# Attention sums that come out negated, with their minimum as the exponentials' bias

## The chip, the cores and the metric

The kernel runs on one core of one Trainium2 chip. The metric is device time in microseconds (us) of one execution; the kernel before was timed in three runs. The profile and the trace are of one more execution, taken by the hardware profiler. TensorE is written PE, VectorE DVE, ScalarE ACT, GpSimd POOL and SyncE SP, as the profile does; PEld is TensorE's weight load.

## The reference, cut to what matters

The network is a first block (an RWKV-7 group and an mLSTM group side by side, then a gated feed-forward stage) and a second block of two layers, 1,024 tokens of 1,024 features, all in float32. The change lies in the second block's attention. Each layer projects its input into three branches: A, four heads with a forgetting bias; B, six heads of a mixture of dilated windows; C, six query heads in a window of 128 with a learned sink per head. For a block of 128 queries and one head each branch computes a softmax over keys:

```
A:  s = q.k * scale + c_q - c_k          (c = cumulative sum of log_sigmoid(gate), c_q is the same for a whole row)
B:  s = q.k * scale + log(number of patterns that reach this key), masked
C:  s = q.k * scale, masked to the window; the sink is one more column with no value
p = exp(s - max(s)) / sum(exp(s - max(s)))      y = p @ v
```

The branch outputs are gated, projected, mixed, projected again and added to the stream; a norm ends the network.

## The kernel before

All engines' programs are written by hand, with semaphores between them; nothing reorders them. Activations lie as eight tiles of 128 features by 1,024 tokens. A float32 product is made of three PE passes over split operands (`hH`, `hL`, `wH`, `wL`); POOL splits each weight slot that SP loads (lines 688 and 690), and line 943 is the product itself (`col_gemm`).

Each layer runs a gate stage (24 gate tiles in ten periods, PE line 1650, the weights' splits on POOL in lines 834 to 855), then the attention, then a merge. In the second gate period and the fourth the forgetting rows are made beside it by DVE in `gate_rows` and `gate_sums` (lines 3686 to 3703): four rows of 1,024 log-gates and their running sum, `lrows`, which ACT sends to memory; before the heads of branch A they are spread over all partitions into `cMe` and `cMo`, and `mask_bias` lays the causal mask on every second block.

The attention takes two heads at a time, a `head_pair`: two pairs of A, three of B, three of C in each layer, so 16 in all: 4 of A, 6 of B, 6 of C. A pair has eight query blocks n = 0 to 7 with two heads j = 0, 1, so 16 pieces. In A and B piece n is 128 queries by (n + 1) * 128 keys; in C it is 128 by 256 (128 for n = 0). For each n:

- PE: `scores(n)` (line 1740) makes the score products in PSUM banks 0 to 3. Before `scores(n)` PE waits on the semaphore `at_max` until both pieces of block n - 1 have been read, and for the tensors it reads. Through n = 3 and in C the first scores stand between pieces of the next weight products (line 943); for A and B, n = 4 to 7 stand by themselves, with `transposes` (line 1767) and `values` (line 1785).
- DVE: `maxima(n)` (line 3790 on). For each head one `tensor_tensor_reduce` (line 3811) adds the bias to the scores, writes the sums to `sc` and keeps their largest; on the chip it is two instructions, the sum itself and a read of the accumulator into `stat`. DVE then waits on `at_ttr` for its own read, and a 128x1 instruction turns the maximum into the bias of the exponentials: a multiplication by -1 (line 3818), in C with the larger of maximum and sink (line 3816). That instruction increments `at_max`.
- ACT: `exponentials(n)` (line 2689) waits for `at_max`, writes exp(sc + bias) in place and sums each row.
- PE transposes the exponentials into PSUM, ACT (`copy_transposed`, line 2709, in C line 2700) and DVE (line 3835, in C line 3828) copy them to `pt`, and PE multiplies them with the values. DVE does its share of the copies and the output gate (lines 3856 and 3861) between its sums, in the order written.

Of the kernel before, what the change touches and what calls it, by code (L numbers as in the profile page):

```python
# [20 lines left out]
ALU = mybir.AluOpType  # L21
ACT = mybir.ActivationFunctionType

P = 128
# [4 lines left out]
LAYERS = 2  # L29
# [62 lines left out]
VEC = {}  # L92
# [51 lines left out]
def build(nc, xin, vec, w_lora, consts, cmask, rope, lnm, band, ws, park, out):  # L144
    with ExitStack() as ctx:
# [36 lines left out]
        def sem(name):  # L182
            if name in LATER:
                name = LATER[name][0]
            if name not in sems:
                sems[name] = ctx.enter_context(nc.semaphore(name))
            return sems[name]
# [20 lines left out]
        pv = at("pv", EX, [P, NV_CHIP])  # L208
# [15 lines left out]
        def colr(name, k):  # L224
            return pv[:, bass.ds(VEC[name] + k, 1)]
# [161 lines left out]
        lnM = at("lnM", XA + 7 * TILE, [P, T])  # L387
# [3 lines left out]
        bandT = at("bandT", EX3 + 4 * TILE, [P, 2 * P])  # L391
        S_MAX, S_NEG, S_DEN, S_SINK, S_REC = range(5)
        stat = at("stat", EX3 + 4 * TILE + 2048, [P, 5, 16])
        rec_rows = at("rec_rows", EX3 + 4 * TILE + 2432, [16, P])
        recT = at("recT", YL, [P, KT, T])
        cM = [at("cMe", YH + 2 * TILE, [P, 2, T]), at("cMo", YH + 4 * TILE, [P, 2, T])]
# [65 lines left out]
        def bank(b, n=1):  # L462
            return ps[:, b:b + n, :].rearrange("p b n -> p (b n)")
# [1583 lines left out]
        def _(act):  # L2047
# [631 lines left out]
            def head_pair(br, L, i, first):  # L2679
                pi = L * 8 + i + first  # L2680
                last, even = pi * 16, pi * 8

                def exponentials(n):
                    c0, c1, _ = columns(br, n)
                    buf, b = (SC[0], band_slot(n)) if br == "C" else (SC[n % 2], 0)
                    for j in range(2):
                        s = 2 * n + j
                        act.wait_ge(sem("at_max"), last + s + 3)
                        act.activation(buf[:, j, b + c0:b + c1], buf[:, j, b + c0:b + c1], ACT.Exp,  # L2689
                                       bias=stat[:, S_NEG, s:s + 1], accum_out=stat[:, S_DEN, s:s + 1]  # L2690
                                       ).then_inc(sem("at_exp"), 1)

# [32 lines left out]
                else:  # L2725
                    slots = head_slots(L, br, i)
                    if br == "B":
                        act.wait_ge(gemm_done[0], slots[0][1] + 1)
                        raw = L * 14 + i * 2 + 2 * first
# [45 lines left out]
                if br == "C":  # L2775
                    act.wait_ge(sem("at_max"), last + 18)
                    act.sem_inc(sem("gate"), 1)
                    for j in range(2):
                        ins = act.activation(stat[:, S_SINK, j:16:2], stat[:, S_NEG, j:16:2], ACT.Exp,
                                             bias=colr("sink", L * 6 + i + 3 * j))  # L2780
# [52 lines left out]
        def _(dve):  # L2833
            own = Count(sem("dve_own"))
# [10 lines left out]
            st = Count(sem("m_step"))  # L2845
# [456 lines left out]
            M_STEPS = st.n  # L3302
# [381 lines left out]
                keys(L, 0)  # L3684

            def gate_rows(L):
                st = Count(sem("m_step"), L * 4 + M_STEPS)
                raw, work, ones = [r[0:4, :] for r in lrows]
                st.on(dve.memset(ones, 1.0))
                st.on(dve.tensor_tensor(raw, raw, grows[0:4, :], ALU.mult))  # L3690
                st.wait(dve)
                st.on(dve.tensor_scalar(raw, raw, pv[0:4, VEC["forget_b"] + L:VEC["forget_b"] + L + 1], None, ALU.add))
                st.wait(dve)
                dve.scalar_tensor_tensor(out=work, in0=raw, scalar=-1.0, in1=raw, op0=ALU.mult, op1=ALU.max
                                         ).then_inc(sem("gate_abs"), 1)
                return st

            def gate_sums(L, st):
                raw, work, ones = [r[0:4, :] for r in lrows]
                dve.wait_ge(sem("gate_log"), 2 * L + 4)  # L3700
                st.on(dve.scalar_tensor_tensor(out=raw, in0=raw, scalar=0.0, in1=work, op0=ALU.min, op1=ALU.subtract))
                st.wait(dve)
                dve.tensor_tensor_scan(work, ones, raw, 0.0, ALU.mult, ALU.add).then_inc(sem("gate_rows"), 1)

            def rope(L, n, a_raw, turned, source, rot, raw, dst):

# [44 lines left out]
            def head_pair(br, L, i, first):  # L3751
# [18 lines left out]
                def mask_bias():  # L3770

                    dve.wait_ge(sem("bB_ready"), 128 + (L * 2 + i + 1) * 64)
                    for q in range(2):
                        masked, bare = [rows[:, :, :].rearrange("p j (b e t) -> p e j b t", e=2, t=P)[:, q]
                                        for rows in (cM[q], cM[1 - q])]
                        dve.tensor_tensor(masked, bare, cst[:, C_NEG, :].unsqueeze(1).unsqueeze(1).to_broadcast([P, 2, KT // 2, P]),
                                          ALU.subtract).then_inc(sem("bias_masked"), 1)

                if br == "A" and i:
                    mask_bias()  # L3780
# [5 lines left out]
                def maxima(n):  # L3786

                    c0, c1, _ = columns(br, n)
                    buf, b = (SC[0], band_slot(n)) if br == "C" else (SC[n % 2], 0)
                    for j in range(2):  # L3790
                        s = 2 * n + j
                        if n >= buffers:

                            dve.wait_ge(sem("at_T"), pi * 16 + s + 1 - 2 * buffers)
                        dve.wait_ge(sem("at_S"), pi * 16 + s + 1)
                        if br == "A" and j == 0:
                            if n < 2:
                                dve.wait_ge(sem("bias_masked"), (L * 2 + i) * 2 + n + 1)
                            else:
                                dve.wait_ge(sem("bB_copied"), bias_copies(L, i) + n - 1)  # L3800
                        if br == "A":
                            bias, op = cM[n % 2][:, j, c0:c1], ALU.subtract
                        elif br == "B":
                            bias, op = lnM[:, P * (7 - n):P * (7 - n) + c1], ALU.add
                        else:
                            bias, op = bandT[:, c0:c1], ALU.add
                        mx = stat[:, S_MAX, s:s + 1]

                        dve.sem_inc(sem("gate"), 1)
                        o = score_bank(br, n, j)  # L3810
                        dve.tensor_tensor_reduce(buf[:, j, b + c0:b + c1], bank(0, 4)[:, o + c0:o + c1], bias, 1.0, -3e38, op,  # L3811
                                                 ALU.max, mx).then_inc(sem("at_ttr"), 1)
                        dve.wait_ge(sem("at_ttr"), pi * 16 + s + 1)
                        neg = stat[:, S_NEG, s:s + 1]
                        if br == "C":
                            ins = dve.tensor_scalar(neg, mx, colr("sink", L * 6 + i + 3 * j), -1.0, ALU.max, ALU.mult)
                        else:
                            ins = dve.tensor_scalar(neg, mx, -1.0, None, ALU.mult)  # L3818
                        ins.then_inc(sem("at_max"), 1)

                def copy_transposed(n):
                    c0, c1, _ = columns(br, n)
# [149 lines left out]
            def last_adds():  # L3972
# [30 lines left out]
                for e in range(KT):  # L4003
                    scale(1, e)

            for name, n in (("at_max", 2), ("at_y", 1), ("a_yL", 1), ("sg_ready", 1), ("sg_raw", 1)):
                dve.sem_inc(sem(name), n)
            for L in range(LAYERS):
# [170 lines left out]
```

## Time and profile before

| what | value |
|---|---|
| times of three runs | 3413.94, 3416.67 and 3421.68 us, median 3416.67 |
| span of the profiled execution, first to last instruction | 3412.5 us; its own time beyond the span is not recorded, the median lies 4.2 us above the span |
| PE busy | 3254.9 us, 95% |
| DVE busy | 1971.0 us, 58% |
| POOL busy | 1622.7 us, 48% |
| ACT busy | 1055.3 us, 31% |
| granted PE clock, mean | 0.985 |

Busy time is what an engine spends in instructions; the rest of the span it waits or issues. An engine with a share near the whole span can still lose time in its waits, and these the trace lists by the instruction that ended them. In the rows a start is in us from the span's first instruction, followed by the duration; `[1.35 <-DVE stat L3818]` means that the engine stood still for 1.35 us before this row and that the instruction on the right of the arrow ended it.

### The profile page before, as it was taken

The numbers are of one execution on the slowest core, as the hardware profiler recorded it, in microseconds if no ns is written. First come the engines' busy times: TensorE is split into PE (matmuls) and PEld (weight loads), VectorE is DVE, ScalarE is ACT, GpSimd is POOL, SyncE is SP. The second block draws the span as 40 slices with busy tenths as digits, with TensorE's granted clock in tenths as the row PEclk, the third lists the DMA queues.
The fourth block names the chain that finished last, engine by engine and source line by source line (L and its number), as shares of the span: only waits on it lengthen the run. The fifth ranks groups of instructions, "written<-read, shape, count | busy, mean of one in ns | idle before, by whom it ended". The sixth has DMA issues, their size and how long they took to land.

```text
span 3412.5 us, 55095 instructions
## 1 busy us (share of the span) xinstructions
PE 3254.9 (95%) x22070; PEld 2604.8 (76%) x22070; DVE 1971.0 (58%) x2678; ACT 1055.3 (31%) x1725; POOL 1622.7 (48%) x903
## 2 busy tenths in 40 slices
PE   7999789898999999999999999999999999999997
PEld 6878688687888888787877777678878877776786
DVE  7445644648877777883344554566752256444665
ACT  4212344223323333344332232320343233322301
POOL 3333334146777676657822222257478422222475
PEclk9999899999999999999999999999999999999998
DMA  3121100221111111112331211143223311111332
GB/s 137 44 91 44 56 4 4 85 83 53 53 55 41 54 55 55 50 62 99 143 107 44 56 52 47 38 163 121 99 105 106 119 45 50 43 44 50 136 124 87
DMA packets 88252, 247.68 MB, mean 73 GB/s; under 512 B 13072, under 2 KB 24048, under 8 KB 86144
## 3 DMA queue, kind: packets, MB, share of 16 engines
q1 hardware_dynamic: 69664, 189.34, 16.5%
q10 hardware_dynamic: 18400, 55.63, 5.0%
q8 instruction: 142, 2.33, 0.3%
q14 instruction: 46, 0.38, 0.0%
HBM read 191.28 MB, written 42.12 MB: 68 GB/s over the span
## 4 chain that ended last, share of the span: by engine, by line
PE 85%; DVE 8%; ACT 2%; issue 2%; POOL 2%; DMA 0%; DVEq 0%; POOLq 0%; SPq 0%; ACTq 0%
PE ps L943 30%; PE ps L1480 11%; PE ps L1650 9%; PE ps L1510 6%; PE ps L1934 5%; PE ps L1955 4%; PE ps L1740 3%; PE ps L1767 3%; PE ps L1785 3%; DVE sc L3811 2%; PE ps L1255 1%; PE ps L1533 1%; PE ps L1231 1%; PE ps L1618 1%; POOL unit_lo L834 1%
## 5 line engine op out<-in xcount | busy, mean ns | idle before, releaser
L688 POOL TENSOR_TENSOR wH<-wraw,pv 128x1024 fp32r<-128x1024 f32 x135 | 267.0, 1978 | 1221.5 <-PE ps L943 1097.7
L943 PE MATMUL ps<-hH,wH 128*128 128x512 f32 x1488 | 473.9, 400 | 26.3 <-DVE hL L3041 11.7
L943 PE MATMUL ps<-hL,wH 128*128 128x512 f32 x1488 | 466.6, 395 | 0.0
L943 PE MATMUL ps<-hH,wL 128*128 128x512 f32 x1488 | 465.2, 394 | 0.0
L3368 DVE TENSOR_TENSOR xT<-ps,xT 128x512 f32<-128x512 f32 x544 | 366.1, 690 | 60.9 <-PE ps L1510 54.8
L690 POOL TENSOR_TENSOR wL<-wraw,wH 128x1024 fp32r<-128x1024 f32 x135 | 353.7, 2620 | 10.6
L943 PEld LDWEIGHTS ps<-hH,wH 128*128 128x128 f32 x1488 | 274.5, 189 | 88.8 <-issue 17.9
L943 PEld LDWEIGHTS ps<-hL,wH 128*128 128x128 f32 x1488 | 277.8, 189 | 59.0 <-issue 1.7
L943 PEld LDWEIGHTS ps<-hH,wL 128*128 128x128 f32 x1488 | 277.7, 189 | 57.5 <-issue 0.3
L2689 ACT ACTIVATE sc<-sc,stat 128x256 f32<-128x256 f32 (+7 forms) x256 | 171.1, 669 | 163.1 <-DVE stat L3818 102.1
L1767 PE MATMUL ps<-cst,sc 128*128 128x128 f32 x900 | 148.7, 285 | 12.5 <-ACT pt L2709 8.4
L1767 PEld LDWEIGHTS ps<-cst,sc 128*128 128x128 f32 x900 | 97.0, 141 | 82.8 <-issue 60.7
L1740 PE MATMUL ps<-kP,qP 64*128 64x256 f32 (+3 forms) x672 | 131.6, 488 | 20.4 <-DVE stat L3818 16.6
L1650 PE MATMUL ps<-mixH,unit_hi 128*128 128x512 f32 x320 | 128.7, 402 | 14.5 <-POOL unit_lo L834 7.6
L1480 PE MATMUL ps<-mixH,unit_hi 128*128 128x512 f32 x336 | 133.8, 398 | 7.0 <-DVE ps L3483 4.1
L1480 PE MATMUL ps<-mixH,unit_lo 128*128 128x512 f32 x336 | 132.7, 395 | 0.0
L1480 PE MATMUL ps<-mixL,unit_hi 128*128 128x512 f32 x336 | 132.7, 395 | 0.0
L1650 PE MATMUL ps<-mixL,unit_hi 128*128 128x512 f32 x320 | 127.9, 400 | 0.0
L1650 PE MATMUL ps<-mixH,unit_lo 128*128 128x512 f32 x320 | 127.7, 399 | 0.0
L1785 PE MATMUL ps<-pt,vtok 128*64 128x128 f32 x1800 | 126.5, 280 | 0.0
L1510 PE MATMUL ps<-gL,wH 128*128 128x512 f32 x320 | 126.5, 395 | 0.0
L1510 PE MATMUL ps<-gH,wH 128*128 128x512 f32 x320 | 124.6, 389 | 0.0
(545 smaller groups left out, 7244.0 us busy)
## 6 DMA issues: line engine op xcount, KB each, us to landing
wraw<-ws SPq DMA_DIRECT2D x158, 512.0 KB, 3.5
gates<-gated SPq DMA_DIRECT2D x48, 512.0 KB, 2.7
sg<-gates SPq DMA_DIRECT2D x16, 1536.0 KB, 6.5
upA<-ws SPq DMA_DIRECT2D x42, 256.0 KB, 3.3
upB<-ws SPq DMA_DIRECT2D x42, 256.0 KB, 2.6
gateA<-ws SPq DMA_DIRECT2D x40, 256.0 KB, 3.5
gateB<-ws SPq DMA_DIRECT2D x40, 256.0 KB, 2.7
xT<-park ACTq DMA_DIRECT2D x2, 4096.0 KB, 12.1
```

Of the source, the lines that this page charges most:

```text
L688: pool.tensor_tensor(wH[:, j, :], wraw[:, j, :], zero, ALU.add).then_inc(w_hi, 1)
L690: pool.tensor_tensor(wL[:, j, :], wraw[:, j, :], wH[:, j, :], ALU.subtract).then_inc(w_ready[j], 1)
L943: mm = pe.matmul(pair(p)[:, half * HALF:(half + 1) * HALF], wp, hp[:, k, half * HALF:(half + 1) * HALF], start=(m == 0 and n == 0), stop=( ...
L1480: mm = pe.matmul(bank(b), wp, xp[:, k0 + k, c0:c0 + HALF], start=(start and k == 0 and n == 0), stop=(k == 3 and n == 2), skip_group_check ...
L1510: mm = pe.matmul(pair((2, 3, 1)[e % 3])[:, half * HALF:(half + 1) * HALF], w[:, 1, e * P:(e + 1) * P], h[:, half * HALF:(half + 1) * HALF] ...
L1650: mm = pe.matmul(bank(banks[b]), wp, xp[:, k0 + k, c0:c0 + HALF], start=(start and k == 0 and m == 0), stop=(k == 3 and m == 2), skip_grou ...
L1740: mm = pe.matmul(outs[j][:, c:e], qP[r, n * P:(n + 1) * P], kP[r, k0 + c - c0:k0 + e - c0], start=True, stop=True)
L1767: mm = pe.transpose(out[:, c:c + P], (SC[0] if br == "C" else SC[n % 2])[:, j, b + c:b + c + P], ident)
L1785: mm = pe.matmul(out[r, :], vtok[:, v + 64 * j:v + 64 * j + 64], pt[:, j, b + c:b + c + P], start=(c == c0), stop=(c + P == c1))
L1934: mm = pe.matmul(pair(p)[:, half * HALF:(half + 1) * HALF], wp, hp[:, k, half * HALF:(half + 1) * HALF], start=(k == k0 and n == 0), stop= ...
L2689: act.activation(buf[:, j, b + c0:b + c1], buf[:, j, b + c0:b + c1], ACT.Exp, bias=stat[:, S_NEG, s:s + 1], accum_out=stat[:, S_DEN, s:s + ...
L3368: ins = dve.tensor_tensor(x, bank(2 * pairs[e % len(pairs)] + half), x, ALU.add)
```

## The change

Every sum is multiplied by -1 as it is made, and the reduction keeps the minimum of the negated sums, which is the negated maximum. It goes straight to the `stat` column that the exponentials read as their bias, and the instruction that makes it increments `at_max`; the 128x1 instruction behind it and the wait on `at_ttr` are gone. The exponential is given a scale of -1. In C the minimum starts from the negated sink, read from a column of `pv`; those 12 columns are filled once, before the first layer. In A the bias was subtracted; since all branches now add, the forgetting rows are multiplied by -1 after their running sum, one 4x1024 instruction in each layer behind the scan, and the mask is added instead of subtracted.

```diff
--- before.py
+++ after.py
@@ -2686,7 +2686,7 @@
                     for j in range(2):
                         s = 2 * n + j
                         act.wait_ge(sem("at_max"), last + s + 3)
-                        act.activation(buf[:, j, b + c0:b + c1], buf[:, j, b + c0:b + c1], ACT.Exp,
+                        act.activation(buf[:, j, b + c0:b + c1], buf[:, j, b + c0:b + c1], ACT.Exp, scale=-1.0,
                                        bias=stat[:, S_NEG, s:s + 1], accum_out=stat[:, S_DEN, s:s + 1]
                                        ).then_inc(sem("at_exp"), 1)
 
@@ -3684,7 +3684,7 @@
                 keys(L, 0)
 
             def gate_rows(L):
-                st = Count(sem("m_step"), L * 4 + M_STEPS)
+                st = Count(sem("m_step"), L * 5 + M_STEPS)
                 raw, work, ones = [r[0:4, :] for r in lrows]
                 st.on(dve.memset(ones, 1.0))
                 st.on(dve.tensor_tensor(raw, raw, grows[0:4, :], ALU.mult))
@@ -3700,7 +3700,9 @@
                 dve.wait_ge(sem("gate_log"), 2 * L + 4)
                 st.on(dve.scalar_tensor_tensor(out=raw, in0=raw, scalar=0.0, in1=work, op0=ALU.min, op1=ALU.subtract))
                 st.wait(dve)
-                dve.tensor_tensor_scan(work, ones, raw, 0.0, ALU.mult, ALU.add).then_inc(sem("gate_rows"), 1)
+                st.on(dve.tensor_tensor_scan(work, ones, raw, 0.0, ALU.mult, ALU.add))
+                st.wait(dve)
+                dve.tensor_scalar(work, work, -1.0, None, ALU.mult).then_inc(sem("gate_rows"), 1)
 
             def rope(L, n, a_raw, turned, source, rot, raw, dst):
 
@@ -3774,7 +3776,7 @@
                         masked, bare = [rows[:, :, :].rearrange("p j (b e t) -> p e j b t", e=2, t=P)[:, q]
                                         for rows in (cM[q], cM[1 - q])]
                         dve.tensor_tensor(masked, bare, cst[:, C_NEG, :].unsqueeze(1).unsqueeze(1).to_broadcast([P, 2, KT // 2, P]),
-                                          ALU.subtract).then_inc(sem("bias_masked"), 1)
+                                          ALU.add).then_inc(sem("bias_masked"), 1)
 
                 if br == "A" and i:
                     mask_bias()
@@ -3799,24 +3801,17 @@
                             else:
                                 dve.wait_ge(sem("bB_copied"), bias_copies(L, i) + n - 1)
                         if br == "A":
-                            bias, op = cM[n % 2][:, j, c0:c1], ALU.subtract
+                            bias = cM[n % 2][:, j, c0:c1]
                         elif br == "B":
-                            bias, op = lnM[:, P * (7 - n):P * (7 - n) + c1], ALU.add
+                            bias = lnM[:, P * (7 - n):P * (7 - n) + c1]
                         else:
-                            bias, op = bandT[:, c0:c1], ALU.add
-                        mx = stat[:, S_MAX, s:s + 1]
+                            bias = bandT[:, c0:c1]
+                        least = colr("qkw", L * 6 + i + 3 * j) if br == "C" else 3e38
 
                         dve.sem_inc(sem("gate"), 1)
                         o = score_bank(br, n, j)
-                        dve.tensor_tensor_reduce(buf[:, j, b + c0:b + c1], bank(0, 4)[:, o + c0:o + c1], bias, 1.0, -3e38, op,
-                                                 ALU.max, mx).then_inc(sem("at_ttr"), 1)
-                        dve.wait_ge(sem("at_ttr"), pi * 16 + s + 1)
-                        neg = stat[:, S_NEG, s:s + 1]
-                        if br == "C":
-                            ins = dve.tensor_scalar(neg, mx, colr("sink", L * 6 + i + 3 * j), -1.0, ALU.max, ALU.mult)
-                        else:
-                            ins = dve.tensor_scalar(neg, mx, -1.0, None, ALU.mult)
-                        ins.then_inc(sem("at_max"), 1)
+                        dve.tensor_tensor_reduce(buf[:, j, b + c0:b + c1], bank(0, 4)[:, o + c0:o + c1], bias, -1.0, least, ALU.add, ALU.min,
+                                                 stat[:, S_NEG, s:s + 1]).then_inc(sem("at_max"), 1)
 
                 def copy_transposed(n):
                     c0, c1, _ = columns(br, n)
@@ -4003,6 +3998,9 @@
                 for e in range(KT):
                     scale(1, e)
 
+            own.on(dve.tensor_scalar(pv[:, VEC["qkw"]:VEC["qkw"] + 6 * LAYERS], pv[:, VEC["sink"]:VEC["sink"] + 6 * LAYERS],
+                                     -1.0, None, ALU.mult))
+            own.wait(dve)
             for name, n in (("at_max", 2), ("at_y", 1), ("a_yL", 1), ("sg_ready", 1), ("sg_raw", 1)):
                 dve.sem_inc(sem(name), n)
             for L in range(LAYERS):
```

On DVE, branch A, block n = 4 and the start of n = 5, before (the `ISA` rows are the sum and the read of its accumulator):

```order
L3811 ISA sc_185,stat<-ps,cMe 128x640 [waits bB_copied,at_T,at_S]
L3811 ISA stat 128x1
L3818 TENSOR_SCALAR stat<-stat 128x1 [waits at_ttr]
L3811 ISA sc_185,stat<-ps,cMe 128x640 [waits at_T,at_S]
L3811 ISA stat 128x1
L3818 TENSOR_SCALAR stat<-stat 128x1 [waits at_ttr]
L3811 ISA sc_186,stat<-ps,cMo 128x768 [waits bB_copied,at_T,at_S]
```

and in the changed program:

```order
L3813 ISA sc_185,stat<-ps,cMe 128x640 [waits bB_copied,at_T,at_S]
L3813 ISA stat 128x1
L3813 ISA sc_185,stat<-ps,cMe 128x640 [waits at_T,at_S]
L3813 ISA stat 128x1
L3813 ISA sc_186,stat<-ps,cMo 128x768 [waits bB_copied,at_T,at_S]
```

The second sum now stands directly behind the first one's read; all other DVE instructions of the pair keep their order. PE, ACT and SP have the same instructions in the same order as before, POOL too but for line numbers.

On DVE in the gate stage, behind the third gate period of each layer, the difference:

```order
 L3701 SCALAR_TENSOR_TENSOR fraw<-fraw,lrows_219 4x1024
 L3703 SCALAR_TENSOR_TENSOR lrows_219<-lrows_220,fraw 4x1024
+L3705 TENSOR_SCALAR lrows_219<-lrows_219 4x1024
 L3639 TENSOR_TENSOR ps<-ps,ecopy 128x512
 L3644 TENSOR_TENSOR gated_214<-ps,grows 128x512
```

The added row waits for the scan above it (line 3703); below it follow the copies of the next gate period.

## Rows read from the trace of the kernel before

**Rows 1.** First part of the page: busy time, share of the span, instructions of each engine.

```profile
PE 3254.9 (95%) x22070; PEld 2604.8 (76%) x22070; DVE 1971.0 (58%) x2678; ACT 1055.3 (31%) x1725; POOL 1622.7 (48%) x903
```

**Rows 2.** Waits of PE, whole span: who waited for whom, us in total, times, longest.

```profile
PE ps L1740 <- DVE stat L3818: 16.6, 21, 1.4
...
PE ps L1740 <- DVE stat L3816: 3.4, 12, 0.4
...
PE ps L943 <- DVE stat L3816: 1.0, 4, 0.3
```

**Rows 3.** PE in order of time, a B pair of the first layer, blocks 5 and 6.

```profile
1926.36 1.56 PE L1740 MATMUL ps<-kP,qP 64*128 64x512 f32 x8 [1.35 <-DVE stat L3818]
...
1929.49 0.77 PE L1767 MATMUL ps<-cst,sc 128*128 128x128 f32 x5 [0.87 <-ACT pt L2709]
1930.57 1.77 PE L1740 MATMUL ps<-kP,qP 64*128 64x512 f32 x8 [0.30 <-DVE stat L3818]
```

**Rows 4.** DVE in order of time, the same B pair, block 4.

```profile
1924.17 0.82 DVE L3811 CUSTOM_DVE_ANT_0 sc<-ps,lnM 128x640 f32<-128x640 f32 x1 [0.65 <-PE ps L1740]
1924.92 0.08 DVE L3811 DVE_READ_ACCUMULATOR2_ANT stat<- 128x1 f32 x1
1925.04 0.15 DVE L3818 TENSOR_SCALAR stat<-stat 128x1 f32<-128x1 f32 x1
1925.29 0.82 DVE L3811 CUSTOM_DVE_ANT_0 sc<-ps,lnM 128x640 f32<-128x640 f32 x1
...
1926.15 0.15 DVE L3818 TENSOR_SCALAR stat<-stat 128x1 f32<-128x1 f32 x1
```

**Rows 5.** DVE in order of time, an A pair, block 4, between its two sums.

```profile
1772.86 0.08 DVE L3811 DVE_READ_ACCUMULATOR2_ANT stat<- 128x1 f32 x1
...
1773.17 0.82 DVE L3811 CUSTOM_DVE_ANT_0 sc<-ps,cMe 128x640 f32<-128x640 f32 x1
```

**Rows 6.** DVE in order of time, one instruction in front of the sum behind it (B pair).

```profile
1905.97 1.23 DVE L3718 TENSOR_TENSOR vtok<-ps,pv 128x1024 f32<-128x1024 f32 x1 [4.99 <-PE ps L1708]
1907.11 0.28 DVE L3811 CUSTOM_DVE_ANT_0 sc<-ps,lnM 128x128 f32<-128x128 f32 x1
```

**Rows 7.** DVE in order of time, a C pair, block 1, from the first read on.

```profile
2144.66 0.08 DVE L3811 DVE_READ_ACCUMULATOR2_ANT stat<- 128x1 f32 x1
2144.78 0.21 DVE L3816 TENSOR_SCALAR stat<-stat,pv 128x1 f32<-128x1 f32 x1
2144.94 0.42 DVE L3811 CUSTOM_DVE_ANT_0 sc<-ps,bandT 128x256 f32<-128x256 f32 x1
...
2145.41 0.21 DVE L3816 TENSOR_SCALAR stat<-stat,pv 128x1 f32<-128x1 f32 x1
```

**Rows 8.** PE in order of time, the same C pair.

```profile
2145.68 0.70 PE L1740 MATMUL ps<-kP,qP 64*128 64x256 f32 x4 [0.26 <-DVE stat L3816]
```

**Rows 9.** The chain that ended last, in the same C pair (start, us, what).

```profile
2156.18 0.60 ACT pt L2700
```

**Rows 10.** DVE by line: count, busy us, mean ns of one, idle before.

```profile
L3818 DVE TENSOR_SCALAR stat<-stat 128x1 f32<-128x1 f32 x160 | 24.6, 154 | 5.7
...
L3816 DVE TENSOR_SCALAR stat<-stat,pv 128x1 f32<-128x1 f32 x96 | 20.6, 214 | 3.4
```

**Rows 11.** DVE in order of time, first layer's gate stage, the scan and what follows.

```profile
1585.98 3.27 DVE L3703 TENSOR_TENSOR_SCAN lrows<-lrows,fraw 4x1024 f32<-4x1024 f32 x1
1591.53 0.70 DVE L3639 TENSOR_TENSOR ps<-ps,ecopy 128x512 f32<-128x512 f32 x1 [2.29 <-PE ps L1650]
```

**Rows 12.** One source line of DVE: ns of one, min/median/max, first and last start.

```profile
L3692 DVE TENSOR_SCALAR fraw<-fraw,pv x2: 1628/1628/1629, 1532.5 to 2504.3; 4x1024 f32<-4x1024 f32 x2
```

**Rows 13.** POOL in order of time, beside the scan of rows 11.

```profile
1587.22 3.10 POOL L834 TENSOR_TENSOR unit_lo<-gateB,unit_hi 128x512 fp32r<-128x512 f32 x1
...
1592.32 1.30 POOL L834 TENSOR_TENSOR unit_lo<-unit_sum,unit_hi 128x512 fp32r<-128x512 f32 x1 [0.74 <-ACT unit_hi L2541]
```

**Rows 14.** The chain that ended last, same gate stage (start, us, what).

```profile
1566.95 59.85 PE ps L1650 x252
```

## Prediction

> **What bounds the kernel now.** The page's first lines come first: PE is busy for 95% of the span, every other engine for 58% or less [rows 1]. So a microsecond saved on DVE counts only where PE stands still for it. The second view is therefore PE's list of waits. Three of its entries end with the instruction that the change removes [rows 2]: `scores` waits for line 3818 (A and B) 21 times, 16.6 us; `scores` waits for line 3816 (C) 12 times, 3.4 us; the product that follows a C pair's scores waits for line 3816 four times, 1.0 us. Together 21.0 us, 0.6% of the span: the change can't win more from these waits, however much work it takes from DVE. The third view is PE and DVE in order of time at such a wait, to see how much of it goes.
>
> In a B pair PE waits 1.35 us before `scores(5)`, 0.87 us for ACT's copy before the second `transposes(4)`, and 0.30 us before `scores(6)` [rows 3]. The ten pairs of A and B all repeat this, so 20 of the 21 waits are these two: 10 x (1.35 + 0.30) = 16.5 of the 16.6 us. The last one is some tenths at most, and I leave it out.
>
> **What is removed: 256 small instructions and their waits.** Line 3818 takes 154 ns 160 times, line 3816 takes 214 ns 96 times [rows 10]: 45 us of DVE, most of it beside a busy PE. What counts is one step: the two sums of a block, from PE's scores to the `at_max` that lets PE go on.
>
> B [rows 4]. The first sum's read starts at 1924.92, the negation 0.12 later, the second sum another 0.25 later: 0.37 from read to sum. With the negation gone the second sum needs only the engine. How soon can it follow? In [rows 6] a sum starts 0.09 us before the instruction in front of it has ended (1905.97 + 1.23 = 1907.20 against 1907.11), although the same semaphore instruction stands between them. So I take it that the second sum starts as the read ends, 0.08 after its start: 0.29 saved. The dear end is that it follows the read as it now follows the negation, 0.25 after: 0.12 saved. Behind the second sum `at_max` comes at the end of the negation, 1926.15 + 0.15 = 1926.30, and PE starts at 1926.36; it will come at the end of the read. The read stands 0.12 ahead of the negation and takes 0.08, so it ends at 1926.11: 0.19 saved. One B step: 0.48, dear end 0.31.
>
> A [rows 5]. From read to sum 0.31, to become 0.08: 0.23 saved, dear end 0.12; and 0.19 at the end. One A step: 0.42, dear end 0.31.
>
> Now the sum over PE's waits. The wait before `scores(5)` is longer than a step's saving, so all of that arrives: 4 x 0.42 + 6 x 0.48 = 4.6 us. The copy that PE waits for next starts from transposes behind `scores(5)`, so this wait moves along and stays as long as it was. Before `scores(6)` DVE is ready two steps earlier (0.84 to 0.96), PE one step earlier (0.42 to 0.48); the difference covers the 0.30 that PE waits, and the wait disappears: 10 x 0.30 = 3.0 us. What is late next there is PE itself, its transposes. From there PE runs on through `scores(7)`, and the gain stays. A and B: 4.6 + 3.0 = 7.6 us; dear end 3.1 + 3.0 = 6.1.
>
> C [rows 7]. From read to sum 0.28, to become 0.08: 0.20. At the end the negation runs to 2145.41 + 0.21 = 2145.62, the read, 0.12 ahead of it and 0.08 long, to 2145.37: 0.25. But the sum now reads its starting value, the sink, from a column, which no sum in the trace does. The nearest rows are the two small instructions, one with such a column and one without: 214 against 154 ns [rows 10]. I charge 0.06 per sum: a step saves 0.33 (dear end 0.06 + 0.19 = 0.25; free end 0.45). In each C pair PE waits three times. Before `scores(2)` it is about 0.25 us [rows 8], all of it gained: 6 x 0.25 = 1.5 us. Before `scores(6)`, the other six waits, 1.9 us in all, nothing: behind them PE needs exponentials that ACT makes after a copy, and that copy starts from PE's transposes in front of `scores(6)` (the chain of waits runs through it, [rows 9]). PE would only wait there instead. The last wait, in four of the six pairs, 1.0 us [rows 2], lies behind the last sums and goes: 1.0 us. C: 2.5 us, dear end 2.4, free end with the other six 4.4.
>
> **What is added.** The forgetting rows get one 4x1024 instruction in each layer, behind the scan. A like one, line 3692, takes 1.63 us [rows 12]. The scan ends at 1585.98 + 3.27 = 1589.25, and DVE then stands still for 2.29 us until PE releases its next copy at 1591.53 [rows 11]. So the instruction ends by about 1590.9 with 0.6 us to spare; nothing waits behind it, and ACT sends the rows off only behind the next gate period. Cost zero; without that cover it would be 2 x 1.63 = 3.3 us. A second cover is POOL: beside the scan a POOL subtraction takes 3.10 us instead of 1.30 [rows 13], yet PE runs through that stretch for 59.85 us without a break [rows 14]. The Trainium skill, SBUF — State Buffer, section SBUF: two separate sides, says that VectorE and GpSimd take one pair of ports as an exclusive lock, so that the loser stands still for a whole instruction. The slow subtraction fits that; the rule speaks against the added instruction, which would hold POOL once more, and the same 3.3 us would be its bound.
>
> The 12 negated sinks are one 128x12 instruction before the first layer. Line 3818 is the nearest row, 0.15 us; with its wait I count 0.3, and no cover. The exponential's scale, the other sign of the mask and add for subtract change no count and no size: sums with add (`lnM`) and with subtract (`cMe`) both take 0.82 us for 640 columns [rows 4, 5]. They count zero.
>
> Sum: 7.6 + 2.5 - 0.3 = 9.8 us gain; dear end 6.1 + 2.4 - 0.3 = 8.2, with the added rows uncovered 4.9; free end 7.6 + 4.4 - 0.3 = 11.7. The profiled span was 3412.5 us, so I expect one near 3402.7. The median of the runs lies 4.2 above that span, and nothing outside the span changes: 3416.67 - 9.8 = **3406.9 us**.
>
> **Rivals.**
> *Half is given back.* The waits for ACT's copies take over where the DVE waits end: only the first wait of A and B (dear end, 10 x 0.31 = 3.1) and C's first (1.5) arrive, 4.6 us less 0.3: 3412.4 us. For it: this is what happens before C's `scores(6)`. Against it: before `scores(6)` of A and B the copy is already waited for, and still 0.30 us of DVE wait follows [rows 3].
>
> *Only the instruction's own time goes.* The second sum may wait for the read in full, and the removed wait be free in any case. Then a step saves two negations' durations, 0.31, which is the dear end: 8.2 us, 3408.5 us. [Rows 4] speak against it, since between the read's end (1925.00) and the second sum (1925.29) lie 0.14 us besides the negation's 0.15, and [rows 6] show an overlap. The Trainium skill, VectorE: DVE Perf Modes, section The DRAIN you can't avoid, states just this rule: the next instruction starts when the pipe is empty, semaphore or not, and only the number of instructions counts. The overlap in the rows disagrees with it.
>
> *Slower: the new sum runs at a lower rate.* Add, times -1, minimum, is a form that the trace does not have. At least four sums of 0.82 us or more in each A and B pair lie between PE's waits: 10 x 4 x 0.82 = 33 us. A sum longer by 30% eats the gain. The slowest DVE row for 1,024 columns is the scan, 3.27 us against 1.23 for a product [rows 11, 6], a factor of 2.66: 1.66 x 33 = 55 us more, 3462 us. Against it: add and subtract run at the same rate, and the multiplication by 1.0 is there already.
>
> **How the numbers follow.** Forecast 60%, 3404 to 3409 us; only the instruction's own time 15%; half given back 17%; added rows uncovered 4% (3.3 us later than the forecast, 3410.2); slower 4%. The three runs of before lie 7.7 us apart, so the median alone moves the result by some 3 us. The free end less that is 3402.0, half given back with half of it on top 3413.9: the range is 3402 to 3414. A measurement of this kernel can tell about 0.2%, 6.8 us, from no change. The forecast exceeds that by 3.0 us, the second case by 1.4, the third stays below: faster 0.66, same 0.30, slower 0.04.
>
> **What would show it.** In the changed kernel's trace: the second sum starts about 0.08 us after the first one's read; PE's wait before `scores(5)` is near 0.85 us and the one before `scores(6)` gone; the wait for ACT's copy between them is as long as now; C's waits before `scores(2)` are gone and those behind `scores(6)` longer; PE's stretch in the gate stage has no break. I am wrong if sums of 640 columns take longer than 0.82 us, if the second sum comes 0.25 us or more after the read, or if PE's wait before `scores(6)` stands.

## The result and the profile after

The changed kernel took 3398.24 us (median of four runs, 3393.71 to 3400.67) against 3416.52 us before beside it (3413.94 to 3421.68): a ratio of 0.9944, 95% interval 0.993 to 0.9958. That is 18.3 us faster, about twice the forecast gain of 9.8 us, and below the range of 3402 to 3414. The direction and, in the main, the mechanism came out as forecast; the size did not. The profiled execution's span is 3397.4 us, 15.1 less than before, at a granted clock of 0.986 (before 0.985).

First the busy time of the changed kernel (us, share of the span, instructions), to be read against [rows 1].

```profile
PE 3249.8 (96%) x22070; PEld 2602.4 (77%) x22070; DVE 1924.7 (57%) x2425; ACT 1041.1 (31%) x1725; POOL 1621.2 (48%) x903
```

DVE has 253 instructions less (256 taken out; one for the sinks and two for the rows put in) and 46 us less work. PE has the same 22070 instructions; its idle time, the span less the busy time, fell by 10.0 us (157.6 to 147.6), and its busy time by 5.1. How busy time can fall with the same work is told in the part on the prediction. PE's list of waits in the changed kernel (who waited for whom, us in total, times, longest) answers [rows 2].

```profile
PE ps L1767 <- ACT pt L2709: 8.4, 10, 0.9
PE ps L1740 <- DVE stat L3813: 8.1, 11, 0.8
...
PE ps L1767 <- ACT sc L2689: 6.3, 8, 1.3
```

The waits of `scores` for DVE fell from 16.6 + 3.4 us to 8.1 (line 3813 is the sum now), that of the C pairs' next product from 1.0 to nothing. The wait for ACT's copy is what it was before: 8.4 us, 10 times. The third entry grew: this is what C gives back. Before, these two entries for ACT were

```profile
PE ps L1767 <- ACT pt L2709: 8.4, 10, 0.9
...
PE ps L1767 <- ACT sc L2689: 3.9, 7, 1.3
```

DVE in order of time, changed kernel, the B pair and block of [rows 4]:

```profile
1921.65 0.82 DVE L3813 CUSTOM_DVE_ANT_0 sc<-ps,lnM 128x640 f32<-128x640 f32 x1 [0.65 <-PE ps L1740]
1922.40 0.08 DVE L3813 DVE_READ_ACCUMULATOR2_ANT stat<- 128x1 f32 x1
1922.40 0.82 DVE L3813 CUSTOM_DVE_ANT_0 sc<-ps,lnM 128x640 f32<-128x640 f32 x1
1923.15 0.08 DVE L3813 DVE_READ_ACCUMULATOR2_ANT stat<- 128x1 f32 x1
```

The second sum starts with the first one's read, at 1922.40, not 0.08 behind it as forecast; before it came 0.37 behind it. PE in order of time in the same pair answers [rows 3]:

```profile
1923.29 1.56 PE L1740 MATMUL ps<-kP,qP 64*128 64x512 f32 x8 [0.79 <-DVE stat L3813]
...
1926.42 0.77 PE L1767 MATMUL ps<-cst,sc 128*128 128x128 f32 x5 [0.87 <-ACT pt L2709]
1927.11 1.77 PE L1740 MATMUL ps<-kP,qP 64*128 64x512 f32 x8
```

The wait before `scores(5)` went from 1.35 to 0.79 us, the one before `scores(6)` is gone, the copy's wait between them stands at 0.87. Now a C pair: DVE at the block of [rows 7].

```profile
2138.57 0.48 DVE L3813 CUSTOM_DVE_ANT_0 sc<-ps,bandT,pv 128x256 f32<-128x256 f32 x1 [2.05 <-PE ps L1740]
2138.97 0.08 DVE L3813 DVE_READ_ACCUMULATOR2_ANT stat<- 128x1 f32 x1
2138.97 0.48 DVE L3813 CUSTOM_DVE_ANT_0 sc<-ps,bandT,pv 128x256 f32<-128x256 f32 x1
2139.38 0.08 DVE L3813 DVE_READ_ACCUMULATOR2_ANT stat<- 128x1 f32 x1
```

A sum that starts from a column takes 0.48 us where it took 0.42: the 0.06 that was charged. PE of the same pair, around `scores(6)` and at the pair's end:

```profile
2150.01 0.70 PE L1740 MATMUL ps<-kP,qP 64*128 64x256 f32 x4
2151.35 0.41 PE L1767 MATMUL ps<-cst,sc 128*128 128x128 f32 x2 [0.63 <-ACT sc L2689]
...
2154.24 0.44 PE L1767 MATMUL ps<-cst,sc 128*128 128x128 f32 x2
2154.47 0.73 PE L943 MATMUL ps<-hH,wH 128*128 128x512 f32 x2
```

`scores(6)` no longer waits, but the transposes behind it wait 0.63 us for ACT's exponentials, where the trace of before has 0.32:

```profile
2157.41 0.41 PE L1767 MATMUL ps<-cst,sc 128*128 128x128 f32 x2 [0.32 <-ACT sc L2689]
```

The gain is given back there, as forecast. The wait before `scores(2)` went in five of the six C pairs. In the first C pair of the second layer 0.21 of its 0.24 us stay, in all three profiled executions of the changed kernel: DVE's sum starts there 1.26 us after `scores(1)`, against 0.90 in the pair shown. No row shows why.

**Where the time went.** The two layers' attention can be cut out of the trace: from a layer's first `scores` to its last transposes, lines 1740 and 1767. The lines' own view gives both ends (ns of one, min/median/max; first to last start). First layer, before:

```profile
L1740 PE MATMUL ps<-kP,qP x336: 269/481/694, 1753.6 to 2240.0; 64*128 64x256 f32 x62, 64*128 64x512 f32 x60, 64*128 64x128 f32 x26, 64*128 64x384 f32 x20
L1767 PE MATMUL ps<-cst,sc x450: 270/273/333, 1760.8 to 2244.1; 128*128 128x128 f32 x150
```

and after:

```profile
L1740 PE MATMUL ps<-kP,qP x336: 269/480/694, 1753.2 to 2232.3; 64*128 64x256 f32 x62, 64*128 64x512 f32 x60, 64*128 64x128 f32 x26, 64*128 64x384 f32 x20
L1767 PE MATMUL ps<-cst,sc x450: 270/273/332, 1760.3 to 2236.4; 128*128 128x128 f32 x150
```

2244.1 - 1753.6 = 490.5 us became 2236.4 - 1753.2 = 483.2; the second layer's 490.8 became 483.5. Together 14.6 us. This measure came out the same within 0.1 us in three profiled executions of the changed kernel, so the experiments are read by it beside their times. The kernel before was profiled once. Outside the attention the two spans differ by 0.5 us only (2431.2 and 2430.7).

### The profile page after: what moved, and what is told of

Its sections match the earlier page's. It is cut to its first block and busy times, and to the rows that moved or that the text cites. A ratio compares the mean times of both kernels' runs of the same rounds, so it can differ in the third digit from the quotient of the medians.

```text
span 3397.4 us, 54842 instructions
## 1 busy us (share of the span) xinstructions
PE 3249.8 (96%) x22070; PEld 2602.4 (77%) x22070; DVE 1924.7 (57%) x2425; ACT 1041.1 (31%) x1725; POOL 1621.2 (48%) x903
## 3 DMA queue, kind: packets, MB, share of 16 engines
q1 hardware_dynamic: 69664, 189.34, 16.6%
## 5 line engine op out<-in xcount | busy, mean ns | idle before, releaser
L1767 PE MATMUL ps<-cst,sc 128*128 128x128 f32 x900 | 148.7, 285 | 14.7 <-ACT pt L2709 8.4
L1650 PE MATMUL ps<-mixH,unit_hi 128*128 128x512 f32 x320 | 127.9, 400 | 14.7 <-POOL unit_lo L834 7.8
```

Source lines behind the costliest of these rows:

```text
L1650: mm = pe.matmul(bank(banks[b]), wp, xp[:, k0 + k, c0:c0 + HALF], start=(start and k == 0 and m == 0), stop=(k == 3 and m == 2), skip_grou ...
L1767: mm = pe.transpose(out[:, c:c + P], (SC[0] if br == "C" else SC[n % 2])[:, j, b + c:b + c + P], ident)
```

## Experiments

Each kernel was timed beside the kernel before. "Attention" is the sum of both layers' stretches, cut out as above; the last column is the difference of the medians.

| kernel | median us | ratio, 95% interval | attention us | attention, difference | time, difference |
|---|---|---|---|---|---|
| before (first trace) | | | 981.3 | | |
| changed, first | 3398.24 | 0.993 to 0.9958 | 966.7 | -14.6 | -18.3 |
| after_again | 3400.04 | 0.9933 to 0.996 | 966.7 | -14.6 | -16.6 |
| after_b | 3396.13 | 0.9929 to 0.9957 | 966.6 | -14.7 | -19.8 |
| late | 3401.23 | 0.9936 to 0.9963 | 966.9 | -14.4 | -15.4 |
| early | 3416.82 | 0.9987 to 1.0005 | 980.1 | -1.2 | +0.2 |
| only_A | 3410.49 | 0.9975 to 0.9994 | 976.5 | -4.8 | -5.4 |
| only_B | 3410.00 | 0.9966 to 0.9987 | 974.7 | -6.6 | -6.1 |
| only_C | 3410.02 | 0.9973 to 0.9992 | 977.0 | -4.3 | -6.1 |
| none | 3416.19 | 0.9986 to 1.0004 | 981.6 | +0.3 | +0.1 |
| read_wait | 3409.54 | 0.997 to 0.9988 | 974.9 | -6.4 | -7.1 |
| filler | 3398.62 | 0.9938 to 0.9967 | 967.1 | -14.2 | -17.3 |
| swap | 3395.63 | 0.9916 to 0.9943 | 961.9 | -19.4 | -20.5 |
| swap_b | 3395.74 | 0.9927 to 0.9955 | 961.9 | -19.4 | -20.2 |

**The same kernel again.** Two runs of the changed kernel beside others. First:

> The changed kernel once more, against the kernel before in more rounds. Its profiled span was 15.1 us shorter, of which the attention of the two layers holds 14.1. If that is all, the median gain is 14 to 16 us (ratio 0.9953 to 0.9959). If something outside the attention gives more, as the median difference of 18.3 us suggests, the ratio stays near 0.9946.

Second:

> The changed kernel once more, beside the three that follow. Same time as in its other runs on every theory: 3398 to 3402 us; PE's list shows 8.1 us on DVE's sums in A and B and 6.3 us on ACT's exponentials.

The gain repeats: 16.6 and 19.8 us on the times, 14.6 and 14.7 in the attention. (The 14.1 in the first expectation is not what the cut above gives.) The first came out at its second case, a ratio of 0.9946. In the second, PE's list has the two figures that were expected, but the median of 3396.13 us lies below the 3398 to 3402.

**Which sums pay.** The theory: only the sums that PE stands waiting for count, in blocks 4 to 6 of A and B and blocks 1 and 7 of C. The rival: the gain follows the number of instructions taken away. `late` has the new form in those blocks alone (84 of 256 sums), `early` in all others; the rows and sinks are negated in both.

```diff
+def negated(br, n):
+    return n in ((1, 7) if br == "C" else (4, 5, 6))        # early: not in
...
+                        if negated(br, n):
                             dve.tensor_tensor_reduce(..., bias, -1.0, least, ALU.add, ALU.min, neg).then_inc(sem("at_max"), 1)
+                            continue
+                        (otherwise the sum, the wait and the 128x1 instruction of before, with add)
```

> The new sums only where PE was seen to wait for them: blocks 4, 5, 6 of the A and B pairs and blocks 1 and 7 of the C pairs, 84 of 256 sums; the other 172 have the old form with its small instruction and wait. Theory of steps (only DVE's time between PE's scores and the release of the next scores counts): nearly the whole gain, 13 to 15 us. Rival of the count (each removed instruction gives back its own share): 84/256 of the gain, 5 us.

> The complement: the old form in blocks 4, 5, 6 of A and B and 1 and 7 of C, the new one in the other 172 sums. Theory of steps: 0 to 1.5 us faster than before. Rival of the count: 10 us.

A third of the sums brings 14.4 of the 14.6 us, the other two thirds 1.2. The rival by count falls. The two add up to 1.0 us more than the whole; 0.35 of that is the single wait that is told under the branches, which both contain.

**Which branch pays.** The new form in one branch alone, the old one in the other two; `negated` reads `br == "A"` and so on, and in `only_B` and `only_C` branch A keeps its subtraction and rows without the sign.

> New sums in branch A alone, the rows and sinks negated as in the change. The theory that each step of a pair that PE waits for pays by itself: four pairs by the 0.93 us that the trace showed for one, 3.7 us faster than the kernel before; with B alone and C alone it adds up to the whole change. Rival, that half of it is given back at the copies: 4 x 0.42 = 1.7 us.

> The change in branch B alone (6 of 16 pairs); A and C in the old form, the forgetting rows with their old sign. From the distance of one B pair to the next in the two traces, 76.25 us before and 75.14 after: 6 x 1.1 = 6.6 us faster. By the prediction's sum it would be 6 x 0.78 = 4.7 us.

> The change in branch C alone (6 pairs); A and B in the old form. From the two traces: one C pair to the next 40.46 us before and 39.68 after, so 4 pairs x 0.8 and 2 last pairs with 0.3, 3.8 us faster. By the prediction's sum 2.5 us. If the copy on ACT that PE waits for in this branch takes everything back, 0.

The attention came out 4.8, 6.6 and 4.3 us shorter, together 15.7, 1.1 more than the whole change. B was near what I expected (6.6), A and C above it. Half given back would have been 1.7 us in A; it falls.

Most of the 1.1 is one wait that doesn't come from the form of the sums. In the trace of before, in the first A pair of the second layer, DVE stands still before the second sum of block 6 for 0.39 us in which it waits for nothing that the profile shows ("issue"):

```profile
2746.36 1.09 DVE L3811 CUSTOM_DVE_ANT_0 sc<-ps,cMe 128x896 f32<-128x896 f32 x1 [0.39 <-issue]
```

PE waits for it before `scores(7)`: this is the twenty-first wait of [rows 2]. In `only_B`, `only_C`, `none` and `early` that sum has the old form too, and there `scores(7)` comes 0.35 us earlier all the same. So 0.35 us stand in the difference of the whole change without being owed to the new sums, and the three branches together count them three times, 0.7 us too often.

**Whether the additions cost anything.** In `none` the rows and sinks are negated and the mask is added, but every sum has the old form (`negated` is always false).

> Only what the change adds and turns round: the forgetting rows negated behind the scan, add instead of subtract in A and in the mask, the column of negated sinks filled but not read; all 256 sums in the old form with their small instruction. The prediction counted 0.3 us slower. If the negated rows are not covered, 3.3 us slower; if something here were the source of the gain outside the attention, faster by some 3 us.

0.1 us on the times, 0.3 in the attention: nothing that can be told, since single blocks of `none` gain or lose up to 0.4 us against the one trace of before. The trace of the changed kernel shows the cover that the forecast named. DVE beside the first layer's scan, to be read with [rows 11]:

```profile
1585.50 3.27 DVE L3703 TENSOR_TENSOR_SCAN lrows<-lrows,fraw 4x1024 f32<-4x1024 f32 x1
1588.80 1.60 DVE L3705 TENSOR_SCALAR lrows<-lrows 4x1024 f32<-4x1024 f32 x1
1591.05 0.70 DVE L3639 TENSOR_TENSOR ps<-ps,ecopy 128x512 f32<-128x512 f32 x1 [0.65 <-PE ps L1650]
```

and POOL beside it [rows 13]:

```profile
1586.75 3.11 POOL L834 TENSOR_TENSOR unit_lo<-gateB,unit_hi 128x512 fp32r<-128x512 f32 x1
1589.82 1.74 POOL L855 TENSOR_TENSOR unit_sum<-gateA 128x512 f32<-128x512 f32 x1
```

The added instruction takes 1.60 us, and DVE still waits 0.65 us for PE behind it. A POOL row beside it stretches to 1.74 us, but less than the one beside the scan. The Trainium skill, SBUF — State Buffer, section SBUF: two separate sides, lets VectorE and GpSimd shut each other out of shared ports; the stretched rows fit that. PE did not wait for them: behind the scan its next idle time is 0.84 us at 1643.47, and the trace of before has 0.83 at the same place, 1643.94.

**Instruction or wait?** Two things were removed from between the two sums: a 128x1 instruction and a wait on DVE's own read. `read_wait` puts back the wait alone, behind every sum:

```diff
                                                  stat[:, S_NEG, s:s + 1]).then_inc(sem("at_max"), 1)
+                        dve.wait_ge(sem("at_max"), pi * 16 + s + 3)
```

> The changed kernel with one wait put back: behind each sum DVE waits for the read of its accumulator, so the second sum can't start beside the read; the small instruction stays away. Theory of steps: the second sum starts 0.2 to 0.3 us behind the read's start instead of with it, the first PE wait grows by that, 2 to 4 us of the gain are lost, and some 11 to 12 remain. Rival, only the number of instructions counts and a wait between two VectorE instructions is free: nothing is lost, 14 to 16 us remain.

I had the size wrong: it costs 8.2 us of attention (974.9 - 966.7), more than half of the gain. DVE in order of time in `read_wait`, a B pair's block 4:

```profile
1930.47 0.82 DVE L3813 CUSTOM_DVE_ANT_0 sc<-ps,lnM 128x640 f32<-128x640 f32 x1 [0.64 <-PE ps L1740]
1931.22 0.08 DVE L3813 DVE_READ_ACCUMULATOR2_ANT stat<- 128x1 f32 x1
1931.53 0.82 DVE L3813 CUSTOM_DVE_ANT_0 sc<-ps,lnM 128x640 f32<-128x640 f32 x1 [0.22 <-DVE stat L3813]
1932.28 0.08 DVE L3813 DVE_READ_ACCUMULATOR2_ANT stat<- 128x1 f32 x1
```

and PE there:

```profile
1932.41 1.56 PE L1740 MATMUL ps<-kP,qP 64*128 64x512 f32 x8 [1.09 <-DVE stat L3813]
...
1935.54 0.77 PE L1767 MATMUL ps<-cst,sc 128*128 128x128 f32 x5 [0.87 <-ACT pt L2709]
1936.48 1.77 PE L1740 MATMUL ps<-kP,qP 64*128 64x512 f32 x8 [0.17 <-DVE stat L3813]
```

With the wait the second sum comes 0.31 us behind the read instead of with it. PE pays that before `scores(5)` (1.09 against 0.79) and again before `scores(6)`, whose wait is back; I had counted it once. From start to start that is 10 x 0.30 + 4 x 0.28 + 6 x 0.24 = 5.6 us in A and B; the other 2.6 are in C, before `scores(2)` and at the pairs' ends, which I hadn't counted. The Trainium skill, VectorE: DVE Perf Modes, section The DRAIN you can't avoid, says that a semaphore between DVE instructions costs nothing extra; the 0.31 us disagree with it for a sum with a read behind it.

`filler` is the counterpart: the instruction without the wait.

```diff
                                                  stat[:, S_NEG, s:s + 1]).then_inc(sem("at_max"), 1)
+                        dve.tensor_scalar(stat[:, S_MAX, s:s + 1], colr("sink", 0), -1.0, None, ALU.mult)
```

> Changed kernel with one 128x1 multiplication (from a constant column to an unused one) put back behind each sum, without a wait and without a part in at_max. The theory that the wait on the sum's own read was the dear part: the second sum starts 0.15 to 0.25 us after the read, the increment behind the second sum is not delayed, so some 0.2 us per step: 3 to 5 us slower than the changed kernel, less than the 9.5 us that the wait alone costs. The Trainium skill's rule, VectorE: DVE Perf Modes, section The DRAIN you can't avoid, by which only the number of instructions counts: the whole gain goes, equal to the kernel before within 2 us.

It costs 0.4 us of attention and 2.5 us of median (the intervals of `filler` and `after_b` overlap), less than either side expected. The 0.4 is some 0.7 of cost less 0.28, because the odd wait of the first C pair of the second layer is absent in `filler`. DVE in `filler`, the same block:

```profile
1921.55 0.08 DVE L3813 DVE_READ_ACCUMULATOR2_ANT stat<- 128x1 f32 x1
1921.55 0.15 DVE L3815 TENSOR_SCALAR stat<-pv 128x1 f32<-128x1 f32 x1
1921.62 0.81 DVE L3813 CUSTOM_DVE_ANT_0 sc<-ps,lnM 128x640 f32<-128x640 f32 x1
```

Read and small instruction start together, and the sum 0.07 later. So of the 0.37 us that lay between read and sum before, an instruction that waits for nothing accounts for 0.07, and the wait for nearly all of the rest. The rule that only the number of instructions counts falls from this side too. Neither run puts anything behind a block's second sum on the way to `at_max`. There the instruction itself counts: `at_max` now comes with the read, 0.19 us earlier in A and B, of which 0.15 is the instruction's own time. `read_wait`, which keeps this part, keeps 6.4 of the 14.6 us.

**Beyond the change.** In C the exponentials are late because ACT copies first [rows 9]. `swap` is the changed kernel with ACT's next exponentials ahead of that copy:

```diff
-                        if n % 2 == 0:
-                            copy_transposed(n)
                         if n < 7:
                             exponentials(n + 1)
+                        if n % 2 == 0:
+                            copy_transposed(n)
```

> The changed kernel, and in branch C ACT makes the exponentials of block n + 1 before its copy of block n instead of after it. In the changed kernel PE waits for exponentials that stand behind that copy 0.63 us in each of 6 pairs and another 1.26 us in the 2 last pairs, 6.3 us in all. If the copy isn't needed at once, up to 5 us faster than the changed kernel, 19 to 20 us faster than before; if PE then waits for the copy instead, the same as the changed kernel or slower.

> Changed kernel, with ACT's exponentials of block n + 1 ahead of its copy of block n in C. The theory that ACT ends the remaining waits of C: 3 to 5 us faster than the changed kernel beside it, and the 6.3 us of PE's waits on the exponentials absent again. Rival, that this was scatter of the runs: equal to it within 1.5 us.

PE's waits on the exponentials (6.3 us) are gone from the list of `swap`, which shows these that bear on the attention:

```profile
PE ps L1767 <- ACT pt L2709: 8.4, 10, 0.9
...
PE ps L1740 <- DVE stat L3813: 8.1, 11, 0.8
...
PE ps L1785 <- ACT pt L2700: 0.9, 2, 0.5
```

The last is new: PE now waits 0.9 us for that copy. The attention is 4.8 us shorter than in the changed kernel, both times it was profiled. It beats the kernel before (0.9929 and 0.9941). Against the changed kernel the medians side by side don't show it: 3395.74 and 3396.13 us, 0.4 apart, where 3 to 5 were expected. Each run's granted clock, its mean over the span, is on record too, and at equal clock the difference is there: at 0.985 four runs of `swap` average 3394.5 us and five of the changed kernel 3399.7, at 0.984 four and two of them 3396.4 and 3400.7. These are few runs, and the sorting by clock was not forecast.

## Why the prediction was right and wrong

The table sets each term of the sum beside the trace: how much more a block's `scores` gained than the block ahead of it, read off the starts of line 1740 in both traces, pair by pair in both layers.

| term | forecast us | measured us |
|---|---|---|
| A, B before `scores(5)` | 4.6 | 4 x 0.50 + 6 x 0.56 = 5.4 |
| A, B before `scores(6)` | 3.0 | 10 x 0.38 = 3.8 |
| A, B before `scores(7)` | 0 | 4 x 0.05 + 6 x 0.13 = 1.0 |
| first A pair of a layer, before `scores(4)` | 0 | 2 x 0.19 = 0.4 |
| one A pair before `scores(7)`, not owed to the new sums | 0 | 0.35 |
| C before `scores(2)` | 1.5 | 5 x 0.32 + 0.03 = 1.6 |
| C around `scores(6)` | 0 | 0.2 |
| C at the pair's end | 1.0 | 0.50 + 0.42 + 0.42 + 0.45 = 1.8 |
| added work | -0.3 | 0 |

The terms add up to the difference of the attention, 14.6 us, but for rounding; forecast 9.8. **Right:** where most of the gain arises, that the copy's wait moves along unchanged, that C gives back at `scores(6)`, that the sums keep their rate in A and B and cost 0.06 us more in C, that the added rows are covered. The rivals fell: half given back by PE's rows at `scores(6)` and by `only_A`, the removed wait being free by `read_wait` and `filler`, the slower sum by the rows above.

**Wrong, first step:** "I take it that the second sum starts as the read ends, 0.08 after its start". It starts with the read: a step is worth 0.37 + 0.19 = 0.56 in B and 0.31 + 0.19 = 0.50 in A, not 0.48 and 0.42. [Rows 6] had an overlap of 0.09 us and the forecast used only that it exists. This is 0.8 us. The Trainium skill, VectorE: DVE Perf Modes, section Two Vector instructions with no wait between them, makes an instruction that it calls held wait until every earlier one has finished. The equal starts agree with a sum that is not held; the section gives no time for it.

**Wrong, second step,** "Now the sum over PE's waits": it took the idle time that PE's list shows for the price of a wait. The price is more, and the rows above show why. Without a wait the row of `scores(6)` starts at 1927.11, while the transposes ahead of it end at 1926.42 + 0.77 = 1927.19: an undisturbed PE starts 0.08 before the modelled end. So a listed wait of 0.30 [rows 3] cost 0.30 + 0.08 = 0.38. At a C pair's end the overlap is larger. PE before, the end of the pair that is shown above for after:

```profile
2160.30 0.44 PE L1767 MATMUL ps<-cst,sc 128*128 128x128 f32 x2
2161.05 0.73 PE L943 MATMUL ps<-hH,wH 128*128 128x512 f32 x2 [0.32 <-DVE stat L3816]
```

From start to start 0.75 us, after the change 2154.47 - 2154.24 = 0.23: 0.52 gained from a wait that is listed with 0.32. And a wait of which the overlap leaves little or nothing has no entry in PE's list at all, as before `scores(7)`. The weight loads showed it: PEld in order of time, before, at `scores(5)`, `(6)` and `(7)` of the B pair,

```profile
1926.36 0.30 PEld L1740 LDWEIGHTS ps<-kP,qP 64*128 64x128 f32 x4 [1.59 <-DVE stat L3818]
...
1930.56 0.30 PEld L1740 LDWEIGHTS ps<-kP,qP 64*128 64x128 f32 x4 [0.54 <-DVE stat L3818]
...
1935.25 0.30 PEld L1740 LDWEIGHTS ps<-kP,qP 64*128 64x128 f32 x4 [0.29 <-DVE stat L3818]
```

and after:

```profile
1923.28 0.30 PEld L1740 LDWEIGHTS ps<-kP,qP 64*128 64x128 f32 x4 [1.03 <-DVE stat L3813]
...
1927.11 0.30 PEld L1740 LDWEIGHTS ps<-kP,qP 64*128 64x128 f32 x4 [0.17 <-DVE stat L3813]
...
1931.67 0.30 PEld L1740 LDWEIGHTS ps<-kP,qP 64*128 64x128 f32 x4 [0.17 <-issue]
```

An undisturbed load stands 0.17 us. 1.59 - 1.03, 0.54 - 0.17 and 0.29 - 0.17 are 0.56, 0.37 and 0.12: what the three starts gained. The whole attention shows the same: with the same instructions PE's busy time in it fell from 945.8 to 942.3 us. So of the 14.6 us 11.1 were idle time and 3.5 lay under rows that counted as busy. The claim of 21.0 us as the most that could be won was therefore no bound; it held only because much of the wait before `scores(5)` remains. One path was not in the sum at all: in the first A pair of a layer the transposes ahead of `scores(4)` wait for ACT's exponentials, and these start 0.19 us earlier because the bias is ready earlier. This step, with the waits that the list leaves out and that path, makes up 3.3 of the 4.8 us. Another 0.35 is the twenty-first wait, which the forecast left out and which is not owed to the new sums; the last 0.3 is the charge for the added work that was not due.

**Wrong, in the range:** "the median alone moves the result by some 3 us". The medians differ by 16.6 to 19.8 us in the three comparisons, the attention by 14.6. With 14.6 the forecast's own arithmetic gives 3416.67 - 14.6 = 3402.1 us, just inside the range; the rest of the miss, 3.9 of 8.7 us, lies outside the attention and took the result out of it. Runs of one kernel lie from 4.7 us (`swap_b`) to 16.3 (`only_A`) apart. In the profiled executions the part outside the attention lies anywhere from 2429.7 (`filler`) to 2440.6 us (`read_wait`); the stretch ahead of the first attention alone, which has the same instructions but for one or two on DVE, took 1751.5 (`only_C`) to 1760.8 us (`read_wait`).

Much of this goes with the granted clock. The seven runs of before at a mean clock of 0.986 average 3412.0 us, the 24 at 0.985 3415.7 and the 20 at 0.984 3417.7. Of the changed kernel six runs at 0.986 average 3396.4 us, five at 0.985 3399.7 and two at 0.984 3400.7. At equal clock the two kernels differ by 15.6, 16.0 and 17.0 us, nearer to the attention's 14.6. But six of the 14 runs of the changed kernel had 0.986, and only seven of the 58 of before whose clock is on record.

**What stays open:** why the changed kernel had the higher clock more often, and whether the 1 to 2 us that are left at equal clock are more than scatter.

## What to carry to other kernels

Price a wait by the distance of two starts, disturbed and undisturbed, and look at the weight loads' waits as well as PE's: the idle time that this profile lists is counted from a modelled end and came out too small by the overlap, 0.07 to 0.21 us here. Where an instruction and a wait on its own engine's result go together, test which of the two is dear: between the two sums here it was the wait (0.31 us against 0.07), behind the second one the instruction. A form that leaves the result where it is needed saves both. Only the few places where the bounding engine stands still pay: 84 of 256 edits brought 14.4 of the 14.6 us.

## What the runs showed of the hardware

A sum that keeps a reduction is two instructions, and the next sum starts together with the read of the accumulator (0.00 us), if nothing waits for it. A wait of DVE on its own accumulator read puts the next sum 0.31 us behind that read (`read_wait`), a 128x1 instruction without a wait in the same place 0.07 (`filler`). A sum of 128x256 whose minimum starts from a column took 482 ns on average; the old sum, whose maximum started from a constant, took 424.
